# Layer 1's token mixer in one-pass products on high and low parts, with GpSimd making most of the low parts

## What is computed

```python
p_lat = a_lat @ w_in                         # 1024 -> 512 (f) + 512 (u) + 1024 (ga) + 1024 (gb)
s_ctx = a_ctx @ w_in[:, OFF_SSM:OFF_GA]      # u for the context
y_ctx, y_lat = s5_branch(s_ctx, p_lat[..., OFF_SSM:OFF_GA], ...)   # a scan over time
g_a = jax.nn.sigmoid(p[..., OFF_GA:OFF_GB])
g_b = jax.nn.sigmoid(p[..., OFF_GB:])
y_a = fourier_mix(p[..., :OFF_SSM]) @ w_four
y_b = (y_s @ w_glu_a) * jax.nn.sigmoid(y_s @ w_glu_b)
return (g_a * y_a + g_b * y_b) @ w_out
```

## Time and profile before

| | |
|---|---|
| median of 3 executions | 2174.06 us (2173.55 to 2176.06) |
| the profiled execution | 2175.41 us, span 2173.6 us |
| TensorE matmul busy | 2073.4 us, 95% |
| VectorE busy | 1391.9 us, 64% |
| ScalarE busy | 922.7 us, 42% |
| GpSimd busy | 0.2 us |
| mean granted TensorE clock | 0.978 |

### The profile page before, as it was taken

The page is one execution under the profiler, slowest core; times in us unless marked ns, Lnnn a source line. Parts: engine busy times, 40 slices in busy tenths (PEclk is TensorE's granted clock), DMA queues, the critical chain, the costliest instruction groups (busy, mean ns, idle before and its releaser), DMA issues.

```text
span 2173.6 us, 26208 instructions
## 1 busy us (share of the span) xinstructions
PE 2073.4 (95%) x10136; PEld 1559.4 (72%) x10136; DVE 1391.9 (64%) x1858; ACT 922.7 (42%) x824; POOL 0.2 (0%) x4
## 2 busy tenths in 40 slices
PE   4999899999999999999979999999999999999995
PEld 1455364447777777589878888888888888888884
DVE  6575635662322233273348888888888888888885
ACT  1212112122211221111036667666766767777673
POOL 0000000000000000000000000000000000000000
PEclk8999999989999999999979999999999999999997
DMA  9432785223355423375439989899998989999993
GB/s 370 117 128 113 199 248 220 81 97 116 155 203 216 161 87 125 75 220 148 160 152 356 372 327 376 317 369 349 354 354 332 374 328 369 342 343 355 347 381 138
DMA packets 84588, 536.49 MB, mean 247 GB/s; under 512 B 23040, under 2 KB 50304, under 8 KB 52992
## 3 DMA queue, kind: packets, MB, share of 16 engines
q1 hardware_dynamic: 62688, 513.89, 64.4%
q10 hardware_dynamic: 21792, 21.01, 2.8%
HBM read 516.59 MB, written 18.28 MB: 246 GB/s over the span
## 4 chain that ended last, share of the span: by engine, by line
PE 91%; DVE 3%; DMA 3%; issue 1%; ACT 1%; SPq 0%; DVEq 0%; ACTq 0%
PE ps L1509 21%; PE ps L1833 14%; PE ps L1834 14%; PE ps L1843 14%; PE ps L1518 6%; PE ps L1522 6%; PE ps L1525 6%; PE ps L1442 2%; PE ps L1765 2%; PE ps L1787 1%; DMA ring<-in_w_mod 1%; PE ps L1657 1%; PE ps L1779 1%; PE ps L1665 1%; PE ps L1466 1%
## 5 line engine op out<-in xcount | busy, mean ns | idle before, releaser
L1346 DVE TENSOR_TENSOR WL<-mring,WH 128x2048 fp32r<-128x2048 f32 x340 | 763.6, 2288 | 114.7 <-ACT WH L837 114.0
L837 ACT ACTIVATE WH<-mring 128x2048 fp32r<-128x2048 f32 x340 | 632.6, 1912 | 148.4 <-PE ps L1843 107.3
L1833 PE MATMUL ps<-WH,XGh 128*128 128x512 f32 x896 | 358.8, 400 | 6.8 <-issue 4.2
L1834 PE MATMUL ps<-WH,XGl 128*128 128x512 f32 x896 | 350.9, 392 | 0.0
L1509 PE MATMUL ps<-aT,ring 128*128 128x512 f32 (+1 forms) x768 | 270.6, 513 | 4.0 <-ACT aT L715 4.0
L1509 PEld LDWEIGHTS ps<-aT,ring 128*128 128x128 f32 x768 | 146.9, 193 | 122.4 <-issue 110.4
L1843 PE MATMUL ps<-WL,XGh 128*128 128x512 f32 x896 | 221.5, 390 | 0.0
L1833 PEld LDWEIGHTS ps<-WH,XGh 128*128 128x128 f32 x896 | 169.0, 189 | 42.9 <-issue 5.5
L1834 PEld LDWEIGHTS ps<-WH,XGl 128*128 128x128 f32 x896 | 169.2, 189 | 34.0
L1843 PEld LDWEIGHTS ps<-WL,XGh 128*128 128x128 f32 x896 | 168.2, 188 | 34.8
L1169 DVE TENSOR_TENSOR ringl<-ring,FWH 128x4096 fp32r<-128x4096 f32 (+2 forms) x19 | 73.4, 3864 | 185.1 <-ACT FWH L701 185.1
(11 more groups left out here) (244 smaller groups left out, 2083.8 us busy)
## 6 DMA issues: line engine op xcount, KB each, us to landing
mring<-in_moe_gate SPq DMA_DIRECT2D x58, 2048.0 KB, 9.6
mring<-in_moe_up SPq DMA_DIRECT2D x57, 2048.0 KB, 9.8
mring<-in_moe_down SPq DMA_DIRECT2D x56, 2048.0 KB, 9.8
ring<-in_w_mod SPq DMA_DIRECT2D x24, 2048.0 KB, 8.2
ring<-in_w_in SPq DMA_DIRECT2D x12, 2048.0 KB, 11.7
ring<-in_ffn_gu SPq DMA_DIRECT2D x11, 2048.0 KB, 10.9
cks<-CW ACTq DMA_DIRECT2D x16, 512.0 KB, 3.2
ring<-cks SPq DMA_DIRECT2D x4, 2048.0 KB, 11.6
```

The source lines that it names most:

```text
L837: nc.scalar.activation(WH[buf][:, o], mring[t % MRING][:, o], ACT.Copy).then_inc(high_done, 1)
L1346: V.tensor_tensor(WL[buf][:, o], mring[t % MRING][:, o], WH[buf][:, o].bitcast(F32), ALU.subtract).then_inc(low_done, 1)
L1833: mm(out_, ah, WH[buf][:, o:o + 512], start=(first and q == 0), stop=False)
L1834: mm(out_, al, WH[buf][:, o:o + 512], start=False, stop=False)
```

## The change

In layer 1's mixer the dense products u, f, ga, gb, ya, glub, glua and out become three fp32r matmuls each (`cut_product`). Each of the 11 weight tiles is cut in quarters of 1,024 floats per partition, 44 in all. ScalarE casts a quarter to its high part in a buffer `FWm` of four quarters (`cut_high`); the low part is written over the quarter in the ring: by GpSimd for the first 24 quarters (u, f, ga, gb), by VectorE (`cut_low`) for the other 20. A quarter of w_in or w_out serves one product; one of w_four or the two w_glu tiles serves two. The cast of quarter n waits until the products on quarter n - 4 are done. The activations get high and low parts as well: of the normalised input by ScalarE and VectorE, of the Fourier branch by ScalarE and GpSimd, of y and the mix by ScalarE and VectorE. New buffers are placed over old ones (a low part over its fp32 source, `aTm` over the first half of `GR`).

```diff
+            def cut_high(n):
+                if n >= QUARTERS:
+                    return
+                if n >= 4:
+                    _, done, _, at, _ = place(quarter_last(n - 4))
+                    act.wait_ge(done, at + 1)
...
+                i = stream_at[cut_tiles[n // 4]]
+                act.wait_ge(landed[i % RING], 16 * (i // RING + 1))
+                nc.scalar.activation(quarter_out(n), quarter_in(n, ring[i % RING][:]), ACT.Copy).then_inc(quarter_high, 1)
...
+                if l:
+                    cut_high(0)
+                    cut_high(1)
                 root("ss", l, 0)
                 shift(l, 0)
+                if l:
+                    cut_high(2)
+                    cut_high(3)
                 for m in range(4):
                     stage_u(l, m)
+                    if l:
+                        cut_high(4 + m)
...
                 for m in range(4):
                     evac(("f", l, m), uF[:, m, t0:NT], cols=n)
+                    if l:
+                        cut_high(8 + m)
...
+                if l:
+                    for j in range(4):
+                        cut_high(28 + j)
+                    act.wait_ge(ys_in, 16 * 2 * (l + 1))
+                    for k in range(MB):
+                        nc.scalar.activation(yh[:, k, :], pack[:, k, 0:n], ACT.Copy).then_inc(y_high, 1)
...
+            def cut_low(n):
+                if n >= QUARTERS:
+                    return
+                dve.wait_ge(quarter_high, n + 1)
+                i = stream_at[cut_tiles[n // 4]] % RING
+                V.tensor_tensor(quarter_in(n, ringl[i][:]), quarter_in(n, ring[i][:]), quarter_out(n).bitcast(F32),
+                                ALU.subtract).then_inc(quarter_low_v, 1)
...
                     V.tensor_tensor(G[:, m, t0:NT], G[:, m, t0:NT], bank[:, 0:n_], ALU.mult).then_inc(free, 1)
+                    if l and m % 2:
+                        cut_low(28 + m // 2)
+                if l:
+                    for k in range(MB):
+                        dve.wait_ge(y_high, k + 1)
+                        V.tensor_tensor(yl[:, k, :], pack[:, k, 0:n_], yh[:, k, :].bitcast(F32),
+                                        ALU.subtract).then_inc(y_low, 1)
+                    for j in range(4):
+                        cut_low(32 + j)
...
+        @block.gpsimd
+        def _(pool):
+            for n in range(POOL_QUARTERS):
+                pool.wait_ge(quarter_high, n + 1)
+                i = stream_at[cut_tiles[n // 4]] % RING
+                nc.gpsimd.tensor_tensor(quarter_in(n, ringl[i][:]), quarter_in(n, ring[i][:]),
+                                        quarter_out(n).bitcast(F32), ALU.subtract).then_inc(quarter_low_p, 1)
...
+            def cut_product(name, m, n, xh, xl, cols, highs=None, lows=None):
+                q = quarter_of(name, m)
+                bank = bank_for(pe, (name, 1, m))
...
+                pe.wait_ge(quarter_high, q + 1)
+                for k in range(n):
...
+                    mm(bank[:, 0:cols], wh[:, k, :], xh(k), start=(k == 0), stop=False)
+                for k in range(n):
...
+                    mm(bank[:, 0:cols], wh[:, k, :], xl(k), start=False, stop=False)
+                pe.wait_ge(*quarter_low(q))
+                for k in range(n):
+                    last = mm(bank[:, 0:cols], wl[:, k, :], xh(k), start=False, stop=(k == n - 1))
+                last.then_inc(place((name, 1, m))[1], 1)
```

More of the change, by code:

```diff
@@ L331, in program @@
         mid = ExitStack()
+        mix1 = ExitStack()
+        FWm = sb(mix1, "FWm", [P, 4, SLOT // 4], F32R)
+        mix1.close()
         mix = ExitStack()
@@ L358, in program @@
         par.close()
+        twin = ExitStack()
+        uFx = sb(twin, "uFx", [P, MB, NT], F32R)
+        twin.close()
         uF = sb(mix, "uF", [P, MB, NT])
@@ L420, in program, with quarter_of, quarter_last, quarter_in @@
         moe.close()
+        uFh, uFl = uFx[:, :, 0:SEQ], uFx[:, :, SEQ:NT]
+        yl, yh = packx[:, :, 0:SEQ], packx[:, :, SEQ:NT]
+        Gh, Gl = Gx[:, :, 0:SEQ], Gx[:, :, SEQ:NT]
+        cut_tiles = [("w_in", 1, 1), ("w_in", 1, 0)] + [("w_in", 1, n) for n in (2, 3, 4, 5)]
+        cut_tiles += [("w_four", 1, 0), ("w_glu_b", 1, 0), ("w_glu_a", 1, 0), ("w_out", 1, 0), ("w_out", 1, 1)]
+        QUARTERS = 4 * len(cut_tiles)
+        POOL_QUARTERS = 24
+        def quarter_of(name, m):
+            first = {"u": 0, "f": 1, "ga": 2, "gb": 4, "ya": 6, "glub": 7, "glua": 8, "out": 9}[name]
+            return 4 * first + (m // 2 if name in ("ya", "glub", "glua") else m)
+        def quarter_last(n):
+            i, q = n // 4, n % 4
+            name, m0 = (("u", 0), ("f", 0), ("ga", 0), ("ga", 4), ("gb", 0), ("gb", 4), ("ya", 0), ("glub", 0),
+                        ("glua", 0), ("out", 0), ("out", 4))[i]
+            return (name, 1, 2 * q + 1 if name in ("ya", "glub", "glua") else m0 + q)
+        def quarter_in(n, tile):
+            k = MB if cut_tiles[n // 4][0] in ("w_four", "w_glu_b", "w_glu_a") else KD
+            w, c = tile.rearrange("p (k c) -> p k c", k=k), SLOT // 4 // k
+            return w[:, :, c * (n % 4):c * (n % 4) + c]
+        def quarter_out(n):
+            k = MB if cut_tiles[n // 4][0] in ("w_four", "w_glu_b", "w_glu_a") else KD
+            return FWm[:, n % 4, :].rearrange("p (k c) -> p k c", k=k)
+        def quarter_low(n):
+            return (quarter_low_p, n + 1) if n < POOL_QUARTERS else (quarter_low_v, n + 1 - POOL_QUARTERS)
         mlanded = [sem(f"mlanded{i}") for i in range(MRING)]
@@ L1548, in _ @@
                 sums(l, 0)
-                w = slot(("w_in", l, 1))[:].rearrange("p (k c) -> p k c", k=KD)
-                for m in range(4):
+                if l:
+                    for m in range(4):
+                        cut_product("u", m, KD, lambda k: aTm[:, k, :], lambda k: aTl[:, k, :], NT,
+                                    (a_high, KD) if m == 0 else None, (a_ready, 2 * KD) if m == 0 else None)
+                else:
+                    w = slot(("w_in", l, 1))[:].rearrange("p (k c) -> p k c", k=KD)
+                for m in range(0 if l else 4):
                     product(("u", l, m), [(w[:, k, P * m:P * m + P], aT[:, k, :]) for k in range(KD)],
@@ L1624, in _ @@
                     mod_sums(8)
-                for name, tile in ((("gb", 4),) if l == 0 else (("ga", 2), ("gb", 4))):
+                for name in (("ga", "gb") if l else ()):
+                    for m in range(8):
+                        cut_product(name, m, KD, lambda k: aTm[:, k, CTX:NT], lambda k: aTl[:, k, CTX:NT], SEQ)
+                for name, tile in ((("gb", 4),) if l == 0 else ()):
                     for h in range(2):
@@ L1668, in _ @@
                                 last.then_inc(side_done, 1)
+                if l:
+                    for m in range(8):
+                        cut_product("ya", m, MB, lambda k: uFh[:, k, :], lambda k: uFl[:, k, :], SEQ, (uf_high, 0), (uf_low, 0))
+                    for m in range(8):
+                        cut_product("glub", m, MB, lambda k: yh[:, k, :], lambda k: yl[:, k, :], SEQ, (y_high, 0), (y_low, 0))
+                    for m in range(8):
+                        cut_product("glua", m, MB, lambda k: yh[:, k, :], lambda k: yl[:, k, :], SEQ)
+                    for m in range(8):
+                        cut_product("out", m, KD, lambda k: Gh[:, k, :], lambda k: Gl[:, k, :], SEQ,
+                                    (mix_high, 0) if m == 0 else None, (mix_low, 0) if m == 0 else None)
+                    sums(l, 1)
+                    pe.wait_ge(a_ready, 4 * KD)
+                    continue
                 w = slot(("w_four", l, 0))[:].rearrange("p (k c) -> p k c", k=MB)
```

91 lines of the change are left out of this document (81 added, 10 removed).

## The result

| | before | after |
|---|---|---|
| median | 2175.06 us (4 runs, 2173.55 to 2177.20) | 2249.59 us (4 runs, 2247.02 to 2254.38) |
| ratio | | 1.0327 [1.0304, 1.035] |
| profiled execution | 2175.41 us, span 2173.6 | 2252.12 us, span 2250.2 |
| mean granted TensorE clock | 0.978 | 0.952 |

What follows compares the result with a forecast made beforehand. The prediction took TensorE, busy 95% of the span, to bound the kernel. Its terms (+2.1, +3.1, +36.8, -4.3, +1.7, +9.7) summed to +49.1: 2224.5 us profiled, 2223 as a median, 8-in-10 range 2177 to 2238.

Steps and rivals of the forecast that it cites:

- norm, u, and low parts, to E: Start of layer 1's mixer: norm and u 2.1 us later, the norm's low parts meeting GpSimd's subtractions +3.1.
- scan's length: VectorE's scan beside GpSimd: 16 subtractions each hold it up by their full length, +36.8 us.
- slack and start of the scan: Ahead of Y: the scan's old slack of 4.3 us is taken off the sum.
- Y at a lower clock: Start of Y: first products run at 1.2 GHz after the long wait, +1.7 us.
- tail: From ya to the end of out: 9.7 us longer, though TensorE has 11 us less to do.
- The lock: Scan: GpSimd's subtractions and VectorE's two-operand instructions contend for exclusive SBUF access, costing the scan up to 36.8 us.
- I take the high end, 16 x 2.3: Scan: 16 GpSimd subtractions of 2.3 us each count in full, 36.8 us; the low end was nothing.
- Rival 3: Gates and tail: weight loads make each 256-column fp32r matmul 0.172 us; kernel 2213 us; chance 0.05.
- first Y products at 1.2 GHz after the long wait +1.7: Start of Y: TensorE's first products run at the lower clock after waiting for the scan, +1.7 us.
- Norm to E: Norm, u and f up to the E products: +2.1 us for norm and u, +3.1 for low parts.
- VectorE's turn: glua in the tail: VectorE's work per product takes 1.95 us, hiding TensorE's 1.45, so VectorE is the bound.

Runs made afterwards that it cites:

- e1: Changed kernel with GpSimd's 24 weight subtractions replaced by memsets that write zeros and read nothing; 2212.78 us, 1.0154 of before.
- e5: Changed kernel with everything behind Y in plain fp32 as before, without casts, low parts or the Fourier branch's subtractions; 2245.75 us, 1.0305 of before.
- e2: Changed kernel with GpSimd's 24 weight subtractions replaced by copies of the high part, one operand read instead of two; 2223.41 us, 1.0203 of before.
- e3: Changed kernel with 84 filler matmuls of constants on TensorE during the wait before Y; 2229.41 us, 1.023 of before.
- e8: Changed kernel with ScalarE's first two weight casts put behind the norm's root instead of ahead; 2246.72 us, 1.0296 of before.
- c1: Kernel before with w_glu_b loaded ahead of y's second move and only out in fp32r parts, GpSimd idle; 2176.44 us, 0.9975 of before.
- g1: Changed kernel with plain fp32 gates, w_glu_b loaded ahead of y's second move, and the first two casts behind the root; 2192.50 us, 1.0043 of before.
- e4: Changed kernel with gates ga and gb in plain fp32 on the input's high part, without their casts and GpSimd work; 2196.53 us, 1.0073 of before.
- f1: Changed kernel with filler matmuls before Y, w_glu_b loaded ahead of y's second move, and first two casts behind the root; 2217.70 us, 1.0156 of before.

## What the prediction had right, and the step that failed

All steps are differences from the sums, after less before.

| step | forecast | measured |
|---|---|---|
| norm, u, and low parts, to E | +5.2 | +10.5 |
| scan's length | +36.8 | +35.6 |
| slack and start of the scan | -4.3 | -4.7 |
| Y at a lower clock | +1.7 | +19.6 |
| tail | +9.7 | +11.0 |
| layer 0, unchanged | 0 | +4.7 |
| sum | +49.1 | +76.7 |

The last sum is the difference of the two spans, 76.6.

- **The lock: right, and closer than it deserved.** "I take the high end, 16 x 2.3" was right in the count (16 instructions above 1 us) and in the length taken for the subtraction (2.43 for 2.3), which was the middle of a wide range. The 16 cost 33.8 us for 36.8; the other 1.8 of the 35.6 are the Fourier branch's four subtractions, which the sum did not have (e1 keeps them, and e5, without them, has a scan of 93.3 us). So the two sums agree in part by luck. The row that it was bounded by, VectorE's own lengths, did not decide it; the place of GpSimd's work beside a chain without slack did. The Trainium skill's rule (SBUF — State Buffer, Who interferes with whom) agrees with e1 and e2: a GpSimd instruction that reads contends, one that only writes does not. The same section says that a `tensor_scalar` can contend too, which I did not use: L1237 is one, and took 2.04 us beside GpSimd's subtraction and 0.17 elsewhere.
- **Rival 3: falls.** "The weight load adds" gave 0.172 us per 256-column matmul; I took 0.121. It is 0.117: 24 matmuls of a gate product in 2.80 us (1007.03 to 1009.83). The gates took 45.0, forecast 46.6.
- **The step that failed: "first Y products at 1.2 GHz after the long wait +1.7".** I took Y for a stretch that starts slow and is soon at full clock, as I took u's 512-column matmuls behind the earlier trace rows. The 1.7 is half of some 3.4 us of matmuls, a length that no row gives; the earlier trace rows has 3.25 us of work at 0.50 before u sped up. Nothing was worked out for Y itself. No row of before shows the clock lost ahead of 64-column matmuls: they kept it there (22.0 us at 1.00), and here they did not get it back (41.6 us at 0.50). e3 shows that the step is the clock's alone. Of the 27.5 us by which the profiled sum was off, it holds 17.9 (19.6 less 1.7), and without them the time would lie inside the range. A row of before, outside the mixer, had shown that busy TensorE can stay at the lower level, in the small matmuls of the router (8 columns, then 128):

```profile
1106.00:1114.00 8.00, 7.89 (x37) 0.50 1.00 429
```

- **Norm to E: the mechanism only half seen.** The table load put the root 1.2 us later, as forecast, but VectorE's small instructions of the norm, shut out by GpSimd's first subtractions, were later still (e8: 4.9 us for both). The low parts were forecast at +3.1 (a subtraction and a half of 2.3 us would be 3.45); L1267 took 738 ns each, against 477 in e1, 4.2 us more for sixteen. u's first product waited for them, and the granted clock was 0.50 from 888 to 908 us.
- **The tail: right in its mechanism, with small errors both ways.** ya's seventh product was late for the multiply, glub began at 25.1 of ya's clock (forecast 24.5), and VectorE's turn was above TensorE's. glub ended at 39.4 for 37.7, since it too started at the lower clock, with four matmuls in 1.21 us (1115.80) against some 0.64 at full clock. VectorE's turn, taken as 1.95, was 1.79, and gave most of that back.
- **Layer 0's 4.7 us** are in no step of the change. The profiles spread by 11 us there.

The last line of the forecast's reasoning, that TensorE has less to do in the tail and it is longer all the same, holds for the whole change: some 28 us less of matmul work were on paper, and none came out. In the gates it lay beside the scan; in glub and glua beside VectorE; in u beside the low parts and the repack. Only out had it on the path, which is where c1's profile is some 5 us shorter.

## What to carry to other kernels

In these runs, work moved to an idle GpSimd was free where it read nothing from SBUF, and was not where it read beside two-operand VectorE instructions: price it as nearly one GpSimd instruction's length (2.11 us of 2.43, 0.74 of 1.07) for each GpSimd instruction that meets a chain without slack. Before cheapening TensorE's products, ask for each stretch what ends it; here the scan, VectorE's turn and a DMA ended all but one. A wait ahead of a run of small matmuls can have a second price, the whole run at half the clock, as Y shows; E shows that it need not. Filler matmuls took it away, but must be sized to the wait. And a repair can uncover a cost that the wait had hidden, as in g1.

## What the runs showed of the hardware

- **Y's small matmuls kept the full clock and did not regain it; E's did.** Y is 320 matmul records of 64 columns. At full clock on arrival (before, e3, e4, and f1 after an idle 1.60 us) they took 22.0 us at a granted 1.00. After 3.7, 15.4 and 36.4 us of idle time (e1, e2, after) they took 41.4 to 41.6, and the windows show 0.50 while TensorE was busy 99% of the time. It came back within ya each time. E is 256 records of 64 columns; in e1 it started at 0.50 after 3.14 us of idle time and was back at full clock after some 6 us. The length of the idle time alone does not tell either: after 3.60 us ahead of E the changed kernel was still at 1.00. The Trainium skill (TensorE: Matmul & The Clock Gate, Part 1) says that "activity releases the throttle"; ya, and E in e1, agree with it; for Y 41.6 us of back-to-back matmuls were not enough. Why stays open.
- **VectorE beside GpSimd's subtraction**: an instruction with two operands in SBUF takes up to 2.5 us instead of 0.23; L1255, with one large operand in SBUF and one in PSUM, takes 6.4 us for sixteen with and without it (e8, before).
- **GpSimd on 1,024 elements**: a subtraction 2.43 us, a copy 1.07, a memset 0.95. The Trainium skill's GPSIMD Engine Reference (section 3.1) gives 4,497 ns for a tensor_tensor of 2,048; the estimate by half of that, 2.25, was near.
- **fp32r at 256 columns** costs 0.117 us at full clock, and 256 columns at 2.4 GHz are 0.107: a weight load of the 0.065 us that rival 3 added does not show. At a granted 0.50 it costs 0.213 (1109.79 to 1110.64 for four).
